# Dense up projection with upper part and remainder as one 512-column moving operand, halves added outside TensorE

## The chip, the cores and the metric

One core of a Trainium2 chip runs the whole program in one launch. The metric is device time in microseconds, the median of several executions of the same kernel. Engines are called by their row names: PE (TensorE, the matmuls), PEld (its weight loads), DVE (VectorE), ACT (ScalarE), POOL (GpSimd), SP (SyncE, which issues the weight DMAs).

## The reference, cut to what matters

All data are float32. A two-layer network (with a mixture of experts in its second layer) is followed by a second two-layer network with conditioned norms. Each dense feed-forward stage, five in all, computes

```
def swiglu(h, wg, wu, wd):
    return (jax.nn.silu(h @ wg) * (h @ wu)) @ wd      # D_MODEL = 1024, D_FF = 2816, 256 tokens
```

and is added to the residual. In the second network the conditioning vector is itself a matrix product, `mod = silu_c @ w_ada[layer] + b_ada[layer]`.

## The kernel before

The activations lie transposed, features on the 128 partitions and the T = 256 tokens along the free axis. A product at float32 accuracy is made of three matmuls in the format fp32r: weights and activations are split into an upper part (a rounded copy) and a remainder (value minus copy), and `mm3` (L1697 to L1699) adds upper x upper, upper x remainder and remainder x upper in PSUM. Each of the three has its own weight load, although the first two load the same block `w_hi`.

A dense feed-forward stage is `ffn(f, n)`, with f = 0, 2, 3, 4, 5 (f = 1 would be the experts, which have code of their own). It goes over n = FF = 22 chunks of 128 hidden features. One weight tile of 3072 columns per chunk (2048 for gate and up, 1024 for down) comes from HBM into a ring of four (`ring`), issued by SP when `tile_used` is raised. Per chunk c:

- PE: `up(c)` makes 8 blocks k x 2 (g = gate, up) x 3 = 48 matmuls of 256 columns into one PSUM bank (4 or 5, in turns; gate in columns 0 to 255, up in 256 to 511), and raises `gu_ready`. It is followed by `down(c - 1)`, 8 x 3 = 24 matmuls of 256 columns into banks 0 to 3, which waits for `hid_ready` of chunk c - 1. The order is up(0), up(1), down(0), up(2), down(1), ..., up(21), down(20), down(21). `up(c)` also waits for the split weights of its tile and for `hid_ready` of chunk c - 2, which frees its bank.
- ACT, strictly in program order: L892 copies the upper part of the gate and up weights for chunk c + 1 (in the last chunk L596, `head`, does so for the next stage, where the order asks for it); L901 copies that of the down weights for chunk c, once down(c - 2) is done; L906 waits for `gu_ready` and writes silu of the gate half from PSUM to `sg`.
- DVE, in program order: L1391 (in the last chunk L1048) subtracts for the remainder of the gate and up weights, after L892; L1400 for that of the down weights; then, in f = 0, 2, 3 and 4, blocks of the conditioning product (L1382, one row of 1024 each, with an accumulator read): none in chunk 0, one in each of chunks 1 to 4, two in each of chunks 5 to 20, none in chunk 21; then it waits for `sg_ready`, L1411 multiplies silu by the up half read from PSUM, L1415 copies the result to `hid_hi`, and L1417 subtracts for `hid_lo` and raises `hid_ready`.
- POOL issues the loads of the conditioning rows, each when its slot of four is free.

`sm` is one buffer of four rows of 256: rows 0 and 1 are `sg`, rows 2 and 3 `hid`. After the last chunk come `modulation` (small DVE operations on the finished conditioning), `residual` (DVE adds Y to xT as pairs of blocks of down(21) finish), and the next `norm` (ACT squares, POOL sums, PE sums over partitions in bank 6, called SS).

Of the kernel before, what the change touches and what calls it, by code (L numbers as in the profile page):

```python
# [22 lines left out]
P = 128  # L23
T = 256
D = 1024
KB = D // P
# [81 lines left out]
def build(nc, x_in, wstream, astream, crow, wpool, wrouter, vectors, consts, out):  # L108
# [6 lines left out]
    with ctx:  # L115
        def sb(name, shape, dtype=fp32):
            return ctx.enter_context(nc.sbuf_tensor(name, shape, dtype))
# [8 lines left out]
        xT = sb("xT", [P, KB, T])  # L126
        hT = sb("hT", [P, KB, T])
        cat = hT
        a_hi = sb("a_hi", [P, KB, T], fp32r)
        a_lo = sb("a_lo", [P, KB, T], fp32r)  # L130
        sq = sb("sq", [P, KB, T])
        proj = sb("proj", [P, 21, T])
        branch = sb("branch", [P, 3 * 4 * (16 + T)])
# [102 lines left out]
        normed = sem("normed")  # L236
        h_ready = sem("h_ready")
        gu_ready = sem("gu_ready")
        sg_ready = sem("sg_ready")
        hid_ready = sem("hid_ready")  # L240
        in_ready = sem("in_ready")
# [93 lines left out]

        def chunks_before(f):

# [244 lines left out]
        def _(act):  # L585
# [294 lines left out]
            def ffn(f, n):  # L880
                base, stage = chunks_before(f), FFN_STAGE[f]
                q0, i0 = SPLITS[stage], STARTS[stage]

                def chunk(c, r=0, last=False):

                    s, nx = (i0 + c) % NS, (i0 + c + 1) % NS
                    rt_ = 16 // NS
                    if c and not last:

                        act.wait_ge(gu_ready, r + (base + c))  # L890
                        act.wait_ge(tile_in[nx], r * rt_ + 16 * ((i0 + c + 1) // NS + 1))
                        nc.scalar.activation(w_hi[:, (q0 + c + 1) % 2, 0:UP], ring[:, nx, 0:UP], ACT.Copy)\  # L892
                            .then_inc(hi_ready, 1)
                    if last and f in NORM_AFTER:
                        act.wait_ge(gu_ready, base + c)
                        for half in range(2 if HEADS[NORM_AFTER[f]] in FFN_STAGE else 1):
                            head(NORM_AFTER[f], half, unused=False)

                    act.wait_ge(split_used, r + (q0 + c - 1))
                    act.wait_ge(tile_in[s], r * rt_ + 16 * ((i0 + c) // NS + 1))  # L900
                    nc.scalar.activation(w_hi[:, (q0 + c) % 2, UP:TILE], ring[:, s, UP:TILE], ACT.Copy)\  # L901
                        .then_inc(hi_ready, 1)
                    act.wait_ge(gu_ready, r + (base + c + 1))
                    if base + c >= 2:
                        act.wait_ge(hid_ready, r + (base + c - 1))
                    nc.scalar.activation(sg[:, c % 2, :], ps[:, 4 + c % 2, 0:T], ACT.Silu)\  # L906
                        .then_inc(sg_ready, 1)

                lead, rounds = ffn_loop(n)
                for c in range(lead):  # L910
                    chunk(c)
                    if c == 0 and f in (0, 2, 3):
                        act.wait_ge(crow_in, 16 * ((0, 2, 3).index(f) + 1))
                        nc.scalar.activation(silu_row, silu_row, ACT.Silu).then_inc(silu_row_ready, 1)
                for c in range(lead, n - 1):
                    chunk(c)
                    if f == 2 and c == FINAL_AT:
                        act.wait_ge(final_ss, 1)
                        nc.scalar.activation(norm_s[:, 0, :], SS[:, T:2 * T], ACT.Sqrt, scale=1.0 / D, bias=V("eps"))\
                            .then_inc(final_std, 1)  # L920
                chunk(n - 1, last=True)
# [117 lines left out]
        def _(dve):  # L1039
# [334 lines left out]
            def ffn(f, n):  # L1374
# [10 lines left out]
                def chunk(c, r=0, last=False, blocks=()):  # L1385

                    b = c % 2
                    if c and not last:
                        n_part = 2 * q0 + up_part(c + 1)
                        dve.wait_ge(hi_ready, r * 2 + (n_part + 1))  # L1390
                        nc.vector.tensor_tensor(w_lo[:, (q0 + c + 1) % 2, 0:UP],  # L1391
                                                ring[:, (i0 + c + 1) % NS, 0:UP],
                                                w_hi[:, (q0 + c + 1) % 2, 0:UP], ALU.subtract)\
                            .then_inc(split_ready, 1)
                    if last and f in NORM_AFTER:
                        for half in range(2 if HEADS[NORM_AFTER[f]] in FFN_STAGE else 1):
                            head(NORM_AFTER[f], half)
                    n_part = 2 * q0 + down_part(c, n)
                    dve.wait_ge(hi_ready, r * 2 + (n_part + 1))
                    nc.vector.tensor_tensor(w_lo[:, (q0 + c) % 2, UP:TILE], ring[:, (i0 + c) % NS, UP:TILE],  # L1400
                                            w_hi[:, (q0 + c) % 2, UP:TILE], ALU.subtract)\
                        .then_inc(split_ready, 1)
                    dve.wait_ge(split_ready, r * 2 + (n_part + 1))
                    dve.sem_inc(tile_used, 1)
                    for i in blocks:
                        at = b0 + i
                        ada_block(at, 0, mod_all[:, at:at + 1])
                    dve.wait_ge(sg_ready, r + (base + c + 1))

                    dve.wait_ge(split_used, r + (q0 + c - 1))  # L1410
                    nc.vector.tensor_tensor(hid[:, b, :], sg[:, b, :], ps[:, 4 + b, T:2 * T], ALU.mult)\  # L1411
                        .then_inc(hid_raw, 1)

                    dve.wait_ge(hid_raw, r + (base + c + 1))
                    nc.vector.tensor_copy(hid_hi[:, b, :], hid[:, b, :]).then_inc(hid_top, 1)  # L1415
                    dve.wait_ge(hid_top, r + (base + c + 1))
                    nc.vector.tensor_tensor(hid_lo[:, b, :], hid[:, b, :], hid_hi[:, b, :], ALU.subtract)\  # L1417
                        .then_inc(hid_ready, 1)
# [271 lines left out]
        def _(pe):  # L1690
# [363 lines left out]
            def ffn(f, n, norm_n):  # L2054
# [3 lines left out]
                def up(c, r=0):  # L2058
# [6 lines left out]
                    for k, g in [(k, g) for k in range(KB) for g in range(2)] if c < 2 else \  # L2065
                            [(k, g) for g in range(2) for k in range(KB)]:
                        if c == 0 and g == 0:
                            wait_head(norm_n, k)
                        if c == 1 and (k, g) == (0, 0):
                            pe.wait_ge(second_lo, SECOND_AT[norm_n] + 1)  # L2070
                        if c == 1 and (k, g) == (KB // 2, 0):
                            pe.wait_ge(split_ready, 2 * q0 + up_part(1) + 1)
                        at = (2 * k + g) * P
                        ins = mm3(ps[:, 4 + c % 2, g * T:(g + 1) * T], parts(stage, c, at, at + P),
                                  (a_hi[:, k, :], a_lo[:, k, :]), k == 0 and (c > 1 or g == 0), k == KB - 1)
                    ins.then_inc(gu_ready, 1)
# [373 lines left out]
```

## Time and profile before

| | us |
|---|---|
| median of 3 runs | 2694.66 (2694.05 to 2695.15) |
| the profiled execution: span from first to last instruction | 2690.4 |

The span of the profiled execution is 4.3 us below the median of the runs; what lies around the span is not in the trace. The page gives, for each engine, busy time and its share of the span; the chain that ended last; and groups of instructions by line, with the idle time of the engine before them. A timeline row gives start, duration, engine, line, operation, written and read tiles, shapes, and in brackets how long the engine sat idle before and who released it. Ends of matmuls are modelled; the distance between the starts of two neighbouring matmuls is what one costs in a stream. The granted TensorE clock is given as a share of 2.4 GHz.

### The profile page before, as it was taken

To read this page: it belongs to the slowest core of one execution; us is meant where nothing else is said; L and a number is where in the kernel's file an instruction comes from. 1 tells how busy PE (TensorE), PEld (TensorE's weight loads), DVE (VectorE), ACT (ScalarE), POOL (GpSimd) and SP (SyncE) were. 2 spreads that over 40 slices of the span, in tenths; PEclk is the share of its full clock that TensorE was granted. 3 is DMA by queue.
4 is the path that set the end of the run, shared out by engine and by line. 5 is a ranking of instruction groups with operands and counts; after the bars stand their busy time and mean duration, and the time that the engine had idled before them with its cause. 6 is when DMAs were issued, how large, how long until landed. Compare 5 with 4: busy or idle time off the path is not lost.

```text
span 2690.4 us, 48898 instructions
## 1 busy us (share of the span) xinstructions
PE 2616.0 (97%) x19438; PEld 2463.6 (92%) x19438; DVE 2068.6 (77%) x2783; ACT 1536.7 (57%) x2198; POOL 189.3 (7%) x257
## 2 busy tenths in 40 slices
PE   8999999999999999999999999998999999998999
PEld 8899988999999999999999899986999999887999
DVE  4677766988988898988889778667788787576654
ACT  4643455777777777777777633545433433445432
POOL 2001020000000000000000111012111010021000
PEclk9999998999999999999999999999999999999999
DMA  7277534998989898989899678431587577431452
GB/s 287 112 298 302 203 127 147 331 354 311 359 312 349 320 354 313 351 324 348 321 349 348 262 275 314 172 134 48 212 311 287 218 302 275 165 118 48 165 188 87
DMA packets 76822, 679.22 MB, mean 252 GB/s; under 512 B 8641, under 2 KB 8769, under 8 KB 27969
## 3 DMA queue, kind: packets, MB, share of 16 engines
q1 hardware_dynamic: 55440, 599.10, 60.0%
q0 software_dynamic: 21168, 77.08, 7.1%
q8 instruction: 158, 2.59, 0.4%
q14 instruction: 56, 0.45, 0.1%
HBM read 675.10 MB, written 1.05 MB: 251 GB/s over the span
## 4 chain that ended last, share of the span: by engine, by line
PE 85%; DVE 7%; ACT 4%; issue 2%; DMA 1%; POOL 0%; DVEq 0%; SPq 0%; ACTq 0%; POOLq 0%
PE ps L1697 23%; PE ps L1698 23%; PE ps L1699 23%; PE ps L2222 11%; PE ps L2187 1%; DVE w_parts L1462 1%; PE ps L2231 1%; PE ps L2197 1%; ACT w_parts L927 1%; DMA ring<-wstream 1%; DVE a_lo L1469 1%; DVE xT L1538 1%; ACT sq L609 1%; DVE pT L1070 1%; PE ps L1991 0%
## 5 line engine op out<-in xcount | busy, mean ns | idle before, releaser
L1697 PE MATMUL ps<-a_hi,w_parts 128*128 128x256 f32 x2544 | 727.9, 286 | 13.8 <-DVE a_lo L1089 6.3
L1698 PE MATMUL ps<-a_lo,w_parts 128*128 128x256 f32 x2544 | 720.7, 283 | 0.0
L1699 PE MATMUL ps<-a_hi,w_parts 128*128 128x256 f32 x2544 | 720.5, 283 | 0.0
L1462 DVE TENSOR_TENSOR w_parts<-ring,w_parts 128x1024 fp32r<-128x1024 f32 x448 | 547.9, 1223 | 70.2 <-ACT w_parts L927 68.4
L1697 PE MATMUL ps<-w_parts 128*128 128x256 f32 x1792 | 528.5, 295 | 0.1
L1697 PEld LDWEIGHTS ps<-a_hi,w_parts 128*128 128x128 f32 x2544 | 488.5, 192 | 24.8 <-issue 16.8
L1698 PE MATMUL ps<-w_parts 128*128 128x256 f32 x1792 | 506.1, 282 | 0.0
L1699 PE MATMUL ps<-w_parts 128*128 128x256 f32 x1792 | 505.7, 282 | 0.0
L1698 PEld LDWEIGHTS ps<-a_lo,w_parts 128*128 128x128 f32 x2544 | 488.6, 192 | 1.5 <-issue 1.4
L1699 PEld LDWEIGHTS ps<-a_hi,w_parts 128*128 128x128 f32 x2544 | 488.9, 192 | 0.0
L927 ACT ACTIVATE w_parts<-ring 128x1024 fp32r<-128x1024 f32 x448 | 472.3, 1055 | 2.0 <-DMA ring<-wstream 2.0
L1698 PEld LDWEIGHTS ps<-w_parts 128*128 128x128 f32 x1792 | 342.1, 191 | 8.6
L1697 PEld LDWEIGHTS ps<-w_parts 128*128 128x128 f32 x1792 | 340.8, 190 | 9.3 <-issue 0.3
L1699 PEld LDWEIGHTS ps<-w_parts 128*128 128x128 f32 x1792 | 341.7, 191 | 0.0
L906 ACT ACTIVATE sm<-ps 128x256 f32<-128x256 f32 x110 | 42.2, 384 | 468.1 <-PE ps L1699 467.9
L1469 DVE TENSOR_TENSOR a_lo<-ring,a_hi 128x1024 fp32r<-128x1024 f32 x224 | 273.9, 1223 | 11.8 <-ACT a_hi L934 11.1
L1391 DVE TENSOR_TENSOR w_parts<-ring,w_parts 128x2048 fp32r<-128x2048 f32 x100 | 229.3, 2293 | 59.9 <-ACT w_parts L892 59.8
L934 ACT ACTIVATE a_hi<-ring 128x1024 fp32r<-128x1024 f32 x224 | 237.6, 1061 | 52.1 <-PE ps L2222 51.9
L1698 PE MATMUL ps<-hid_lo,w_parts 128*128 128x256 f32 x880 | 249.0, 283 | 0.0
L1699 PE MATMUL ps<-hid_hi,w_parts 128*128 128x256 f32 x880 | 248.6, 282 | 0.0
L1697 PE MATMUL ps<-hid_hi,w_parts 128*128 128x256 f32 x880 | 246.7, 280 | 0.0
L1124 DVE TENSOR_TENSOR w_parts<-ring,w_parts 128x1536 fp32r<-128x1536 f32 (+1 forms) x85 | 151.2, 1812 | 101.4 <-ACT w_parts L672 97.8
(250 smaller groups left out, 4099.6 us busy)
## 6 DMA issues: line engine op xcount, KB each, us to landing
ring<-wstream SPq DMA_DIRECT2D x378, 1536.0 KB, 8.0
proj<-astream POOLq DMA_DIRECT2D x144, 512.0 KB, 6.1
cst<-consts SPq DMA_DIRECT2D x1, 1700.0 KB, 15.4
vtok<-crow POOLq DMA_DIRECT2D x3, 512.0 KB, 3.9
xT<-x_in SPq DMA_DIRECT2D x1, 1024.0 KB, 5.2
out<-xT SPq DMA_DIRECT2D x1, 768.0 KB, 3.3
proj<-wpool SPq DMA_DIRECT2D x1, 512.0 KB, 15.5
out<-xT SPq DMA_DIRECT2D x1, 256.0 KB, 3.3
```

The lines of the kernel that those rows point to most:

```text
L609: nc.scalar.activation(sq[:, k, :], xT[:, k, :], ACT.Square, scale=both[:, KB + k:KB + k + 1] if n == 5 else D ** -0.5)\
L906: nc.scalar.activation(sg[:, c % 2, :], ps[:, 4 + c % 2, 0:T], ACT.Silu)\
L927: nc.scalar.activation(up_hi[:, n % 2, half * D:(half + 1) * D], ring[:, s, half * D:(half + 1) * D], ACT.Copy).then_inc(xup_hi, 1)
L934: nc.scalar.activation(wd_hi[:, n % 2, :], ring[:, s, UP:TILE], ACT.Copy).then_inc(xdown_hi, 1)
L1124: nc.vector.tensor_tensor(w_lo[:, q, a:b], ring[:, (STARTS[stage] + i) % NS, a:b], w_hi[:, q, a:b], ALU.subtract).then_inc(split_ready, 1)
L1391: nc.vector.tensor_tensor(w_lo[:, (q0 + c + 1) % 2, 0:UP], ring[:, (i0 + c + 1) % NS, 0:UP], w_hi[:, (q0 + c + 1) % 2, 0:UP], ALU.subtract)\
L1462: nc.vector.tensor_tensor(up_lo[:, n % 2, at], ring[:, s, at], up_hi[:, n % 2, at], ALU.subtract).then_inc(xup_lo, 1)
L1469: nc.vector.tensor_tensor(wd_lo[:, n % 2, :], ring[:, s, UP:TILE], wd_hi[:, n % 2, :], ALU.subtract).then_inc(signal, 1)
L1697: mm(o, stationary[0], moving[0], start=start, stop=False, skip_group_check=True)
L1698: mm(o, stationary[0], moving[1], start=False, stop=False, skip_group_check=True)
L1699: return mm(o, stationary[1], moving[0], start=False, stop=stop, skip_group_check=True)
L2222: ins = mm(ps[:, bank + half, :], h[:, b, 0:CAP], w[:, b, half * D // 2:(half + 1) * D // 2], start=c == 0 and i == 0, stop=c == FX - 1 an ...
```

## The change

`a_hi` and `a_lo` become the two halves of one buffer `a_parts`. In four of the five dense stages (`joined(f)`, f = 0, 3, 4, 5; in f = 2 another sum uses bank 6) `up(c)` issues per block k and g one matmul of the stationary `w_hi` block with both halves, 512 columns, and one of `w_lo` with `a_hi`, 256 columns, into the first half: 16 x 2 = 32 matmuls in place of 48. Gate and up have a bank each, 4 and 5 or 6 and 7 in turns. In columns 0 to 255 of a bank stands upper x upper plus remainder x upper, in 256 to 511 upper x remainder. After `gu_ready`, ACT copies columns 256 to 511 of both banks into `sg` and `hid` (512 elements a partition); DVE adds columns 0 to 255 of both banks to them (512 elements); ACT then makes silu of `sg` in place in SBUF; DVE multiplies `sg` and `hid`, both in SBUF. The rest is as before.

```diff
-        a_hi = sb("a_hi", [P, KB, T], fp32r)
-        a_lo = sb("a_lo", [P, KB, T], fp32r)
+        a_parts = sb("a_parts", [P, 2, KB, T], fp32r)
+        a_hi, a_lo = a_parts[:, 0], a_parts[:, 1]
...
+        def joined(f):
+
+            return f != 2
+
+        def added_before(f):
+
+            return chunks_before(f) - (FF if f > 2 else 0)
+
+        def gu_bank(f, c):
+
+            return 4 + 2 * (c % 2) if joined(f) else 4 + c % 2
+
...
+                    if joined(f):
+                        act.wait_ge(gu_ready, r + (base + c + 1))
+                        if base + c >= 2:
+                            act.wait_ge(hid_ready, r + (base + c - 1))
+                        gu = ps[:, gu_bank(f, c):gu_bank(f, c) + 2, :]
+                        nc.scalar.activation(sm[:, c % 2::2, :], gu[:, :, T:2 * T], ACT.Copy).then_inc(gu_copied, 1)
+                        act.wait_ge(gu_added, r + (added_before(f) + c + 1))
+                        nc.scalar.activation(sg[:, c % 2, :], sg[:, c % 2, :], ACT.Silu).then_inc(sg_ready, 1)
+                        return
...
+                    if joined(f):
+                        dve.wait_ge(gu_ready, r + (base + c + 1))
+                        gu = ps[:, gu_bank(f, c):gu_bank(f, c) + 2, :]
+                        dve.wait_ge(gu_copied, r + (added_before(f) + c + 1))
+                        nc.vector.tensor_tensor(sm[:, b::2, :], sm[:, b::2, :], gu[:, :, 0:T], ALU.add)\
+                            .then_inc(gu_added, 1)
                     dve.wait_ge(sg_ready, r + (base + c + 1))
...
-                    nc.vector.tensor_tensor(hid[:, b, :], sg[:, b, :], ps[:, 4 + b, T:2 * T], ALU.mult)\
-                        .then_inc(hid_raw, 1)
+                    if joined(f):
+                        nc.vector.tensor_tensor(hid[:, b, :], sg[:, b, :], hid[:, b, :], ALU.mult).then_inc(hid_raw, 1)
+                    else:
+                        nc.vector.tensor_tensor(hid[:, b, :], sg[:, b, :], ps[:, 4 + b, T:2 * T], ALU.mult)\
+                            .then_inc(hid_raw, 1)
...
+                        if joined(f):
+                            hi, lo = parts(stage, c, at, at + P)
+                            bank = gu_bank(f, c) + g
+                            mm(ps[:, bank, :], hi, a_parts[:, :, k, :], start=k == 0, stop=k == KB - 1,
+                               skip_group_check=True)
+                            ins = mm(ps[:, bank, 0:T], lo, a_hi[:, k, :], start=False, stop=k == KB - 1,
+                                     skip_group_check=True)
+                            continue
```

## Rows read from the trace of the kernel before

**Rows 1.** The page: busy time by engine, and the chain that ended last

```profile
PE 2616.0 (97%) x19438; PEld 2463.6 (92%) x19438; DVE 2068.6 (77%) x2783; ACT 1536.7 (57%) x2198; POOL 189.3 (7%) x257
PE 85%; DVE 7%; ACT 4%; issue 2%; DMA 1%; POOL 0%; DVEq 0%; SPq 0%; ACTq 0%; POOLq 0%
```

**Rows 2.** Windows of the joined stages: length, busy us by engine, PEclk, DMA share, GB/s

```profile
140.00:315.00 175.00, 175.00 (x1461) 175.00 (x1461) 137.39 (x191) 64.41 (x63) 17.36 (x33) 1.00 0.76 286
2496.00:2690.00 194.00, 189.57 (x1578) 189.22 (x1577) 104.49 (x128) 72.52 (x71) 0.00 (x0) 0.99 0.41 153
```

**Rows 3.** Timeline, one chunk of f = 3, ACT: start, duration, line, [idle <- releaser]

```profile
2030.00 0.38 ACT L906 ACTIVATE sm<-ps 128x256 f32<-128x256 f32 x1 [4.69 <-PE ps L1699]
2030.28 1.91 ACT L892 ACTIVATE w_parts<-ring 128x2048 fp32r<-128x2048 f32 x1
...
2038.63 0.38 ACT L906 ACTIVATE sm<-ps 128x256 f32<-128x256 f32 x1 [4.69 <-PE ps L1699]
```

**Rows 4.** Timeline, the same chunk, DVE

```profile
2030.41 0.42 DVE L1411 TENSOR_TENSOR sm<-sm,ps 128x256 f32<-128x256 f32 x1 [0.87 <-ACT sm L906]
2030.87 0.29 DVE L1415 CAST hid_hi<-sm 128x256 fp32r<-128x256 f32 x1
2031.20 0.42 DVE L1417 TENSOR_TENSOR hid_lo<-sm,hid_hi 128x256 fp32r<-128x256 f32 x1
2032.22 2.29 DVE L1391 TENSOR_TENSOR w_parts<-ring,w_parts 128x2048 fp32r<-128x2048 f32 x1 [0.60 <-ACT w_parts L892]
2034.43 1.22 DVE L1400 TENSOR_TENSOR w_parts<-ring,w_parts 128x1024 fp32r<-128x1024 f32 x1
2035.80 1.23 DVE L1382 SCALAR_TENSOR_TENSOR proj<-proj,vtok 128x1024 f32<-128x1024 f32 x1
...
2038.09 0.08 DVE L1382 DVE_READ_ACCUMULATOR proj<-proj,vtok 128x1 f32 x1
```

**Rows 5.** Timeline, PE, matmuls of 256 columns: up ends, down(c - 1), next up

```profile
2038.43 0.28 PE L1697 MATMUL ps<-hid_hi,w_parts 128*128 128x256 f32 x1
...
2041.31 0.28 PE L1697 MATMUL ps<-a_hi,w_parts 128*128 128x256 f32 x1
...
2047.07 0.28 PE L1697 MATMUL ps<-hid_hi,w_parts 128*128 128x256 f32 x1
```

**Rows 6.** Timeline, PE, matmuls of 512 columns in the experts, six in a row

```profile
1272.97 0.63 PE L2222 MATMUL ps<-a_hi,hid_hi 128*128 128x512 f32 x2
1273.44 0.63 PE L2222 MATMUL ps<-a_lo,hid_hi 128*128 128x512 f32 x2
1273.91 0.63 PE L2222 MATMUL ps<-a_hi,hid_lo 128*128 128x512 f32 x2
1274.37 0.81 PE L2231 MATMUL ps<-proj,pT 128*128 128x256 f32 x3
```

**Rows 7.** Timeline, PE, matmuls of 384 columns: the first and last of seven

```profile
1806.33 0.33 PE L1697 MATMUL ps<-w_parts,a_hi 128*128 128x384 f32 x1
...
1807.37 0.33 PE L1697 MATMUL ps<-w_parts,a_hi 128*128 128x384 f32 x1
```

**Rows 8.** Groups by line and form: count, busy us, mean ns, idle before

```profile
L956 ACT ACTIVATE w_parts<-ps 128x512 fp32r<-128x512 f32 x16 | 9.5, 591 | 7.7 <-PE ps L2187 7.7
L803 ACT ACTIVATE a_hi<-hT 128x256 fp32r<-128x256 f32 x32 | 12.6, 416 | 24.0 <-DVE hT L1207 23.9
L1267 DVE TENSOR_TENSOR branch<-ps,cst 128x512 f32<-128x512 f32 x12 | 8.3, 690 | 9.0 <-PE ps L1818 7.7 <-DVE w_parts L1124 1.1
```

**Rows 9.** Timeline, DVE, last chunk of f = 0

```profile
310.11 0.42 DVE L1411 TENSOR_TENSOR sm<-sm,ps 128x256 f32<-128x256 f32 x1 [3.40 <-ACT sm L906]
```

**Rows 10.** Windows at idle stretches of PE and behind them, columns as in rows 2

```profile
73.80:76.10 2.30, 0.20 (x3) 0.08 (x4) 1.73 (x4) 2.30 (x10) 0.00 (x0) 1.00 0.00 0
76.70:80.10 3.40, 3.40 (x15) 2.59 (x16) 2.01 (x2) 3.39 (x11) 0.00 (x0) 0.50 0.02 5
...
376.60:378.80 2.20, 0.09 (x3) 0.02 (x2) 1.62 (x4) 2.20 (x10) 0.00 (x0) 1.00 0.01 4
378.80:382.20 3.40, 3.40 (x28) 2.59 (x28) 2.03 (x2) 3.40 (x8) 0.00 (x0) 1.00 0.00 0
...
423.30:426.20 2.90, 0.03 (x1) 0.00 (x0) 2.29 (x3) 2.83 (x5) 0.00 (x0) 1.00 0.00 0
428.30:431.70 3.40, 3.40 (x17) 3.40 (x17) 3.40 (x5) 0.37 (x1) 0.00 (x0) 0.50 0.02 5
```

**Rows 11.** Timeline, DVE, remainders of the activations for up(0) of f = 0

```profile
125.36 0.42 DVE L1094 TENSOR_TENSOR a_lo<-hT,a_hi 128x256 fp32r<-128x256 f32 x1
...
126.09 0.42 DVE L1094 TENSOR_TENSOR a_lo<-hT,a_hi 128x256 fp32r<-128x256 f32 x1
```

More of the change, by code:

```diff
@@ L238, in build @@
         gu_ready = sem("gu_ready")
+        gu_copied = sem("gu_copied")
+        gu_added = sem("gu_added")
         sg_ready = sem("sg_ready")
```

## The prediction, blind

> **What bounds the kernel now.** I read the page first: PE is busy for 97% of the span and carries 85% of the chain that ended last [rows 1]. That is an average, so I next took the stretches of the joined stages. In them PE is busy throughout, while DVE is busy 137 of 175 us in a stage with conditioning blocks and 104 of 194 us in f = 5, which has none [rows 2]. DVE has room on average; the reader is to see that the room differs by stage. Then I laid out one chunk. Silu starts of neighbouring chunks are 8.63 us apart [rows 3]. PE goes from the start of down(c - 1) through the next up to the following down in the same 8.64 us, without a hole: 72 matmuls at 0.120 us, 2.88 us of down and 5.76 us of up [rows 5]. So PE sets the pace. Its margins are short in one place: DVE finishes the second conditioning block at 2038.17, only 0.46 us before the next silu starts at 2038.63 [rows 3, 4]. ACT begins the next weight copy 0.28 us after silu starts, and not before, as the copy stands behind silu in its order [rows 3].
>
> **What PE saves.** Per block and gate three matmuls of 256 columns, 3 x 119.9 = 359.7 ns, become one of 512 and one of 256. Six matmuls of 512 columns in a row took 1.40 us, 233 ns each [rows 6]. Those of 384 columns took 1.04 us for six, 173 ns each [rows 7]: 13 ns over their 160 ns of columns at 2.4 GHz, as those of 256 are 13 ns over 107. By that the 512 would cost 227 ns. I take 232, near the direct row, so the pair costs 352 ns and saves 7.7 ns; the bounds are 347 (saving 13) and 360 (saving none, if a moving operand in two pieces costs more than one in one piece, which no row shows; I keep a loss beyond that out, because the 256-column matmul is unchanged). Below, I also price 336, a 512 with no extra beyond its columns. At 16 pairs a chunk the saving is 0.12 us, so the PE pace becomes 8.51 us; over 22 chunks 2.7 us per stage, over four stages 10.8 us. Up(0) doesn't give it, since the remainders of the activations come every 0.73 us [rows 11] and a k takes 0.72 already: 4 x 0.12 = 0.5 us less, of which the stages limited by DVE feel little; I charge 0.3.
>
> Section "Back-to-back issue gap" of the Trainium skill's page "TensorE: Matmul & The Clock Gate" gives an isolated matmul its columns over 2.4 GHz plus 2.5 ns: 216 ns for 512, 109 ns for 256. By that the three cost 328 ns and the pair 325 ns, an estimate from the page of a saving of only 3 ns. The trace disagrees with the page on both sizes (120 and 233 ns).
>
> **What ACT and DVE get.** Per chunk ACT gains a copy of 512 elements from PSUM, 0.591 us (the nearest row of that shape), and its silu now reads SBUF, 0.416 for 0.38. DVE gains an addition of 512 elements with PSUM, 0.690 us [rows 8]; its product of two SBUF operands stays at 0.42, as L1417 does [rows 4]. Work alone would fit, but the order matters. Before, the path from up's end to hid_ready was silu, product, cast, subtraction: 1.62 us from the silu's start [rows 3, 4]. Now it is 0.59 + 0.03, 0.69 + 0.03, 0.42 + 0.04, 0.46, 0.33 and 0.42: 3.0 us. The 0.03 is what such a hand-over takes (silu ends at 2030.38, the product starts at 2030.41). In the middle of a stage this is hidden: down(c) starts a whole pace later.
>
> **The loop that the addition closes.** Silu now waits for an addition on DVE, and DVE comes to it only behind the two conditioning blocks of that chunk; the next weight copy on ACT waits behind silu; L1391 on DVE waits for that copy; the blocks of the next chunk stand behind L1391. Before, silu waited for PE alone, so DVE could be late without delaying ACT. Once around: addition 0.69 + 0.03; silu start to weight copy start 0.32 (its 0.42 less the 0.10 of overlap that rows 3 show); copy 1.91 + 0.03; L1391 to L1400 2.21; L1400 to first block 1.37; two blocks 2.29 to the accumulator read, with which the next DVE instruction may start [rows 3, 4]. The sum is 8.85 us. That is 0.34 above the new PE pace and 0.22 above the old one. With one block once around takes 7.70, with none (f = 5) 6.55, so only chunks 5 to 20 of f = 0, 3 and 4 fall behind.
>
> DVE falls behind by 16 x 0.34 = 5.5 us in such a stage. The cover is the distance from hid_ready to down's start: 8.51 less the 3.0 of the path, less 0.20 by which silu starts behind the matmul that follows up [rows 3, 5], less about 0.15 for PE to pick up: 5.15 us. The split weights for up(c + 2) have about the same cover. So PE stands some 0.3 us inside the stage. In the last chunk there are no blocks, and DVE regains 8.51 - 6.55 = 2.0 us; before, it waited 3.40 us there [rows 9]. It is then still about 3.2 us late. Only down(20), 2.88 us, lies between up(21) and down(21), and even an undelayed path needs 0.20 + 3.0 + 0.15 = 3.35 us, 0.4 to 0.5 more than that. PE thus waits about 3.5 us ahead of down(21). Each such stage comes to -2.7 + 0.3 + 3.5 = +1.1 us. In f = 5 it is -2.7 + 0.4 = -2.3 us. Sum so far: 3 x 1.1 - 2.3 + 0.3 = +1.3 us.
>
> **The clock.** A wait of 3.5 us is longer than any now in the trace. The 2.1 us of idle before 76.1 and the 2.9 us before 426.2 were followed by stretches at a granted clock of 0.50 (1.2 GHz), about 0.6 and 2 us after PE had begun again; a like 2.1 us before 378.8 was not [rows 10]. Behind the new wait stands down(21), 2.88 us of dense matmuls, and then the norm. If the clock falls 0.6 to 2 us into it, 0.9 to 2.3 us of that work doubles; the most is half of a 3.4 us stretch, 1.7 us. I take 1.2 per stage, 3.6 in all, with 0 and 5.1 as bounds.
>
> **Costs at nothing.** The conditioning loads on POOL and the ring loads on SP are raised by DVE up to 5.3 us later, but a tile is loaded nearly three paces ahead and DMA is at 76% [rows 2]; if the loads were short, ACT would show waits on `ring`. The table load for silu (it now lies between copy and silu in chunk 0) delays chunk 0, whose hidden part is needed only after up(1). The strided write of `sm` and two more semaphores: nothing. Stage f = 2 and the experts are untouched.
>
> **The forecast.** +1.3 + 3.6 = +4.9 us: 2690.4 becomes 2695.3 in the span, and 2694.66 becomes 2699.6 in the median.
>
> **Rivals.**
> - *The loop as above, but the clock holds.* The 2.1 us before 378.8 speak for it, the length of the new wait against. 2694.66 + 1.3 = 2696.0; at 347 ns a pair (+0.6 a stage with blocks, -4.25 in f = 5) 2692.5.
> - *Slower: the loop is longer than 8.85.* Once the cover is used up, each 0.05 us more costs 3 x 16 x 0.05 = 2.4 us. Its place is the two new hand-overs and the two 512-element reads of PSUM while PE writes beside them; for it speaks that no row shows ACT and DVE reading banks in this way, against it that all its terms are rows with spreads of 0.01 us. At 9.0 us: +4.9 + 7.2, so 2706.8. It is outside 0.2% from 8.86 on.
> - *No saving on PE* (the change doesn't do what it says). With the pair at 360 the sum is 3 x 1.6 + 0.4 + 0.3 = +5.6, with the clock +9.2: 2703.9. By the Trainium skill's 3 ns (pair at 357) it would be 3 x 1.4 - 0.7 + 0.3 = +3.8, with the clock +7.4: 2702.1. Rows 6 speak against both.
> - *Faster: the extra time of a matmul is its weight load, and goes under the 512 columns.* Pair at 336, clock holding: +0.4 in each limited stage, -8.0 in f = 5, +0.3: -6.5, 2688.2. For it: one weight load in three goes. Against: 384 columns still pay 13 ns. Only f = 5 can gain, as the loop holds the others.
>
> **How the numbers follow.** Chances: forecast 0.46, clock holds 0.19, loop longer 0.17, no saving 0.12, faster 0.06. A measurement tells about 0.2%, 5.4 us, from no change. The forecast at +4.9 lies just inside it, with bounds that go over it (1.3 + 5.1 = +6.4), so I split it 0.29 to 0.17; clock holds goes inside; loop longer to slower; of no saving 0.02 lies inside. Faster 0.06, same 0.50, slower 0.44. The range from 2691.5 to 2708.0 leaves out the faster rival, and above it the loop longer than 9.03.
>
> **What would show it.** Right: starts of 512 and 256 in up 232 and 120 ns apart; silu starts 8.85 us apart in the later chunks of f = 0, 3, 4, and 8.51 in f = 5; PE idle about 3.5 us before down(21) in those three and about 0.4 in f = 5; the granted clock at 0.5 right behind. Wrong: silu starts at PE's pace in all stages (a shorter loop, and some -9 us), or waits of up and down from chunk 10 on (a longer one).

## The result and the profile after

The changed kernel takes 2702.82 us (median of 6 runs, 2701.67 to 2705.79) against 2694.68 us of the kernel before in the same rounds (6 runs, 2692.24 to 2695.72): ratio 1.0031, 95% interval 1.002 to 1.0043. It is slower by 8 us. The forecast was 2699.6 with a range of 2691.5 to 2708.0; the time lies in the range, but "within 0.2%" was given the most and "slower" came. The profiled execution has a span of 2700.4 us, 10.0 longer than before. First the page of the kernel after, the same two parts as in [rows 1].

```profile
PE 2611.9 (97%) x18030; PEld 2391.1 (89%) x18030; DVE 2125.4 (79%) x2871; ACT 1578.9 (58%) x2286; POOL 190.3 (7%) x257
...
PE 67%; DVE 19%; ACT 8%; issue 5%; DMA 1%; POOL 0%; DVEq 0%; ACTq 0%; SPq 0%; POOLq 0%
```

The busy shares hardly moved; the chain did. There are 1408 matmuls fewer, PE's share of the chain went down from 85% to 67%, and DVE's up from 7% to 19%. The next view is one chunk in f = 3 of the kernel after, first ACT, then DVE, as in [rows 3, 4].

```profile
2041.24 0.42 ACT L924 ACTIVATE sm<-sm 128x256 f32<-128x256 f32 x1 [5.19 <-DVE sm L1435]
2041.56 1.90 ACT L906 ACTIVATE w_parts<-ring 128x2048 fp32r<-128x2048 f32 x1
2043.37 1.04 ACT L915 ACTIVATE w_parts<-ring 128x1024 fp32r<-128x1024 f32 x1
2044.31 0.58 ACT L922 ACTIVATE sm<-ps 128x512 f32<-128x512 f32 x1
2050.08 0.42 ACT L924 ACTIVATE sm<-sm 128x256 f32<-128x256 f32 x1 [5.20 <-DVE sm L1435]
```

```profile
2040.52 0.68 DVE L1435 TENSOR_TENSOR sm<-sm,ps 128x512 f32<-128x512 f32 x1
2041.69 0.43 DVE L1441 TENSOR_TENSOR sm<-sm 128x256 f32<-128x256 f32 x1 [0.48 <-ACT sm L924]
...
2043.49 2.29 DVE L1414 TENSOR_TENSOR w_parts<-ring,w_parts 128x2048 fp32r<-128x2048 f32 x1 [0.59 <-ACT w_parts L906]
2045.70 1.22 DVE L1423 TENSOR_TENSOR w_parts<-ring,w_parts 128x1024 fp32r<-128x1024 f32 x1
2047.07 1.23 DVE L1405 SCALAR_TENSOR_TENSOR proj<-proj,vtok 128x1024 f32<-128x1024 f32 x1
...
2048.22 1.22 DVE L1405 SCALAR_TENSOR_TENSOR proj<-proj,vtok 128x1024 f32<-128x1024 f32 x1
2049.36 0.08 DVE L1405 DVE_READ_ACCUMULATOR proj<-proj,vtok 128x1 f32 x1
2049.36 0.68 DVE L1435 TENSOR_TENSOR sm<-sm,ps 128x512 f32<-128x512 f32 x1
```

L1435 is the addition, L924 silu, L922 the copy out of PSUM, L906 and L1414 the upper part and the remainder of the next gate and up weights. Silu used to wait 4.69 us for PE [rows 3]. Now it waits 5.2 us for the addition on DVE, and the addition starts the moment the second conditioning block is done, without any idle time. From addition to addition 8.84 us pass. By the starts of these rows that is once around the loop: addition to silu 0.72, silu to weight copy 0.32, copy to L1414 1.93, L1414 to L1423 2.21, L1423 to the first block 1.37, and two blocks to the next addition 2.29. PE would need 8.43 (e2_pe_part_alone below).

To see where the 10 us arise I took the length of each stage from the traces, from the first matmul of its up(0) to the first matmul behind the next norm, less the same in the kernel before (us; f = 0 is 197.55 us there). In brackets stands what the 24 matmuls of down(21) took beyond the 2.76 us of the kernel before, at a lower granted clock, contained in the number ahead of it.

| kernel | f = 0 | f = 3 | f = 4 | f = 5 | all other stretches |
|---|---|---|---|---|---|
| after | +5.6 (2.3) | +4.3 (1.4) | +3.6 (1.6) | -3.6 | +0.1 |
| e1_blocks_behind_add | -3.5 | -3.4 | -3.6 | -3.6 | +6.0 |
| e2_pe_part_alone | -4.2 | -4.1 | -4.3 | -4.1 | +0.8 |
| e3_three_matmuls | +4.7 (1.6) | +3.1 | +2.3 | +0.6 | +4.7 |
| e4_filled_wait | +4.8 | +5.2 | +3.9 | -3.6 | +2.3 |
| e5_row_first | +6.0 (1.6) | +5.3 (1.1) | +3.6 (1.4) | -3.6 | +3.7 |
| e7_filled_seven | +3.3 | +3.1 | +2.4 | -3.7 | +3.1 |
| e8_one_each_side | -3.5 | -3.4 | -3.6 | -3.6 | +5.2 |
| e9_copy_ahead_of_silu | -3.4 | -3.3 | -3.2 | -3.2 | +2.2 |
| e10_row_behind_copies | +6.5 (2.3) | +4.9 (1.1) | +3.5 (1.4) | -3.6 | +2.6 |
| e11_row_and_its_wait | +3.8 (1.5) | +3.3 (1.4) | +4.5 (2.3) | -3.7 | +5.3 |
| e12_three_one_each_side | +0.5 | +0.6 | +0.5 | +0.5 | -1.5 |

The last column is code that no kernel changed. It varies by 7.5 us from trace to trace, so the table is read by its stages. The four stages added up meet the difference of the medians within 3 us in every kernel but e3_three_matmuls, where the median is 5 us higher than they say; what made those 5 us was not found.

### The profile page after: what moved, and what is told of

Read it like the earlier page. It is cut to its first block, busy times and chain, and to the rows that moved or that the text cites. A ratio compares the mean times of both kernels' runs of the same rounds, so it can differ in the third digit from the quotient of the medians.

```text
span 2700.4 us, 46346 instructions
## 1 busy us (share of the span) xinstructions
PE 2611.9 (97%) x18030; PEld 2391.1 (89%) x18030; DVE 2125.4 (79%) x2871; ACT 1578.9 (58%) x2286; POOL 190.3 (7%) x257
## 4 chain that ended last, share of the span: by engine, by line
PE 67%; DVE 19%; ACT 8%; issue 5%; DMA 1%; POOL 0%; DVEq 0%; ACTq 0%; SPq 0%; POOLq 0%
PE ps L1729 15%; PE ps L1730 15%; PE ps L1731 15%; PE ps L2262 11%; DVE w_parts L1414 4%; PE ps L2109 4%; ACT w_parts L906 4%; DVE w_parts L1423 2%; DVE proj L1405 2%; PE ps L2111 2%; DVE sm L1435 1%; PE ps L2227 1%; DVE w_parts L1494 1%; PE ps L2271 1%; PE ps L2237 1%
## 5 line engine op out<-in xcount | busy, mean ns | idle before, releaser
L2109 PE MATMUL ps<-a_parts,w_parts 128*128 128x512 f32 x1408 | 496.4, 395 | 4.1 <-DVE a_parts L1112 3.4
L2111 PE MATMUL ps<-a_parts,w_parts 128*128 128x256 f32 x1408 | 394.0, 280 | 0.0
L1729 PE MATMUL ps<-a_parts,w_parts 128*128 128x256 f32 x1136 | 327.6, 288 | 10.1 <-DVE a_parts L1112 3.1
L1730 PE MATMUL ps<-a_parts,w_parts 128*128 128x256 f32 x1136 | 321.5, 283 | 0.0
L1731 PE MATMUL ps<-a_parts,w_parts 128*128 128x256 f32 x1136 | 321.3, 283 | 0.0
L2109 PEld LDWEIGHTS ps<-a_parts,w_parts 128*128 128x128 f32 x1408 | 263.9, 187 | 64.1 <-issue 6.2
L1501 DVE TENSOR_TENSOR a_parts<-ring,a_parts 128x1024 fp32r<-128x1024 f32 x224 | 273.9, 1223 | 11.5 <-ACT a_parts L957 10.9
L1414 DVE TENSOR_TENSOR w_parts<-ring,w_parts 128x2048 fp32r<-128x2048 f32 x100 | 229.2, 2292 | 63.1 <-ACT w_parts L906 63.1
L957 ACT ACTIVATE a_parts<-ring 128x1024 fp32r<-128x1024 f32 x224 | 237.5, 1060 | 50.5 <-PE ps L2262 50.3
L2111 PEld LDWEIGHTS ps<-a_parts,w_parts 128*128 128x128 f32 x1408 | 265.8, 189 | 0.0
L1729 PE MATMUL ps<-hid_hi,w_parts 128*128 128x256 f32 x880 | 252.8, 287 | 12.3 <-DVE hid_lo L1449 10.1
L2262 PE MATMUL ps<-a_parts,hid_hi 128*128 128x512 f32 x896 | 248.6, 399 | 11.4 <-DVE hid_lo L1586 10.9
L1731 PE MATMUL ps<-hid_hi,w_parts 128*128 128x256 f32 x880 | 251.1, 285 | 0.0
```

The lines of the kernel that those rows point to most:

```text
L957: nc.scalar.activation(wd_hi[:, n % 2, :], ring[:, s, UP:TILE], ACT.Copy).then_inc(xdown_hi, 1)
L1414: nc.vector.tensor_tensor(w_lo[:, (q0 + c + 1) % 2, 0:UP], ring[:, (i0 + c + 1) % NS, 0:UP], w_hi[:, (q0 + c + 1) % 2, 0:UP], ALU.subtract)\
L1501: nc.vector.tensor_tensor(wd_lo[:, n % 2, :], ring[:, s, UP:TILE], wd_hi[:, n % 2, :], ALU.subtract).then_inc(signal, 1)
L1729: mm(o, stationary[0], moving[0], start=start, stop=False, skip_group_check=True)
L1730: mm(o, stationary[0], moving[1], start=False, stop=False, skip_group_check=True)
L1731: return mm(o, stationary[1], moving[0], start=False, stop=stop, skip_group_check=True)
```

## The experiments

All are edits of the changed kernel.

**e2_pe_part_alone.** PE's part without its price: copy and addition are left out, and with them the term upper x remainder of the result.

```diff
-                        nc.scalar.activation(sm[:, c % 2::2, :], gu[:, :, T:2 * T], ACT.Copy).then_inc(gu_copied, 1)
-                        act.wait_ge(gu_added, r + (added_before(f) + c + 1))
-                        nc.scalar.activation(sg[:, c % 2, :], sg[:, c % 2, :], ACT.Silu).then_inc(sg_ready, 1)
+                        nc.scalar.activation(sg[:, c % 2, :], ps[:, gu_bank(f, c), 0:T], ACT.Silu)\
+                            .then_inc(sg_ready, 1)
...
-                        nc.vector.tensor_tensor(sm[:, b::2, :], sm[:, b::2, :], gu[:, :, 0:T], ALU.add)\
-                            .then_inc(gu_added, 1)
...
-                        nc.vector.tensor_tensor(hid[:, b, :], sg[:, b, :], hid[:, b, :], ALU.mult).then_inc(hid_raw, 1)
+                        nc.vector.tensor_tensor(hid[:, b, :], sg[:, b, :], ps[:, gu_bank(f, c) + 1, 0:T], ALU.mult)\
+                            .then_inc(hid_raw, 1)
```

> Only PE's part of the change: matmuls of 512 and 256 columns, but ACT and DVE as in the kernel before (silu and product read columns 0 to 255 of the two banks; no copy, no addition, and the term upper x remainder in columns 256 to 511 is left out of the result). It measures the saving by itself. Loop theory: nothing else stood in the way, so each of the four stages is 21 x 16 x 0.013 = 4.4 us shorter: 2694.7 - 17.5 = 2677. Rival (a 512-column matmul saves less in a long stream than the rows show, 7.7 ns a pair): 2694.7 - 10.3 = 2684.

Measured: 2676.93 us, ratio 0.9939 (0.9922 to 0.9955), as expected. Silu starts are 8.43 us apart in all four stages; each is 4.1 to 4.3 us shorter. The pair is worth 13 ns, not 7.7. The timeline of PE in the kernel after shows how, two pairs from f = 4:

```profile
2119.70 0.40 PE L2109 MATMUL ps<-a_parts,w_parts 128*128 128x512 f32 x1
2119.94 0.28 PE L2111 MATMUL ps<-a_parts,w_parts 128*128 128x256 f32 x1
2120.05 0.40 PE L2109 MATMUL ps<-a_parts,w_parts 128*128 128x512 f32 x1
2120.28 0.28 PE L2111 MATMUL ps<-a_parts,w_parts 128*128 128x256 f32 x1
2120.40 0.40 PE L2109 MATMUL ps<-a_parts,w_parts 128*128 128x512 f32 x1
```

From pair to pair 0.35 us pass. Over the whole stage a 512-column matmul takes 230 ns and the 256-column one behind it 117 ns from start to start (medians; the means are 234 and 117).

**e3_three_matmuls.** ACT's and DVE's part without the saving of PE.

```diff
-                            mm(ps[:, bank, :], hi, a_parts[:, :, k, :], start=k == 0, stop=k == KB - 1,
+                            mm(ps[:, bank, 0:T], hi, a_hi[:, k, :], start=k == 0, stop=False,
+                               skip_group_check=True)
+                            mm(ps[:, bank, T:2 * T], hi, a_lo[:, k, :], start=False, stop=k == KB - 1,
```

> Only ACT's and DVE's part: copy, addition and silu in SBUF as in the changed kernel, but the 512-column matmul is undone into two of 256 into the same columns, so PE's pace is 8.63 again. Loop theory: f = 0, 3 and 4 are held by the loop of 8.85 us and hardly notice, at most 0.7 us each; f = 5 loses its 4.4 us: 2702.8 + 4.4 + about 0.5 = 2708, with silu starts still 8.85 apart. Rival (PE still sets the pace and the loss is in waits at the ends): each of the four stages loses 4.4 us, 2702.8 + 17.5 = 2720.

Measured: 2710.46 us, ratio 1.0064 (1.0047 to 1.008). The stage without blocks loses its whole gain (from -3.6 to +0.6), the three with blocks lose nothing (+4.7, +3.1, +2.3 for +5.6, +4.3, +3.6). They are even shorter, as the clock fell in one of them only: without the numbers in brackets they are +3.1, +3.1 and +2.3 for +3.3, +2.9 and +2.0. Silu stays at 8.85 us. PE doesn't set the pace of f = 0, 3 and 4.

**e1_blocks_behind_add.** The loop is opened on DVE: the conditioning blocks of a chunk are done behind the addition.

```diff
+                        for i in blocks:
+                            at = b0 + i
+                            ada_block(at, 0, mod_all[:, at:at + 1])
                     dve.wait_ge(sg_ready, r + (base + c + 1))
```

The same three lines ahead of the addition are left to f = 2 alone.

> The changed kernel with one edit: in the joined stages DVE does the conditioning blocks of a chunk behind the addition instead of ahead of it. Work and counts are the same. Loop theory (silu waits for an addition that stands behind two blocks, and the weight copy stands behind silu): the two blocks (2.3 us) leave the loop, which falls from 8.85 to about 8.1 us (addition 0.7, blocks 2.3, product, cast and subtraction 1.1, L1414 2.2, L1423 1.4, waits about 0.3), under PE's pace of 8.43. All four stages then run at 8.43, PE waits 0.4 to 0.5 us before the last down, the clock doesn't fall, and each stage is 3.9 us shorter than in the kernel before: 2694.7 - 15.6 = 2679. Rival theory (ACT and DVE have too much work in all, or their reads of PSUM hold up PE, in whatever order): the time stays within 3 us of the changed kernel's 2702.8.

Measured: 2681.49 us, ratio 0.9952 (0.9936 to 0.9969). All work of the change is still there, only its order on DVE differs, and the kernel is 21 us faster than the changed one. The timeline of e1 in f = 0, ACT and DVE:

```profile
204.81 0.60 ACT L922 ACTIVATE sm<-ps 128x512 f32<-128x512 f32 x1 [3.83 <-PE ps L2115]
206.24 0.42 ACT L924 ACTIVATE sm<-sm 128x256 f32<-128x256 f32 x1 [0.82 <-DVE sm L1436]
...
213.25 0.60 ACT L922 ACTIVATE sm<-ps 128x512 f32<-128x512 f32 x1 [3.83 <-PE ps L2115]
```

```profile
205.51 0.69 DVE L1436 TENSOR_TENSOR sm<-sm,ps 128x512 f32<-128x512 f32 x1 [0.99 <-ACT sm L922]
206.12 1.22 DVE L1405 SCALAR_TENSOR_TENSOR proj<-proj,vtok 128x1024 f32<-128x1024 f32 x1
```

ACT's copy waits for PE again, DVE's addition has 0.99 us to spare, and the pace is 8.44.

**e8_one_each_side** leaves the first block ahead of the addition and puts the second behind it (`blocks[:1]` and `blocks[1:]` in the two loops of e1).

> The changed kernel with the first conditioning block of a chunk ahead of the addition, as it was, and only the second, in chunks 5 to 20, behind it. Loop theory: once around is the addition 0.69 + 0.03, silu 0.32, weight copy 1.94, L1414 2.21, L1423 1.37, one block 1.15, that is 7.7 us on ACT's side; on DVE's side, blocks and all, 8.1 to 8.2. Both are under 8.43, so the chunks with two blocks run at PE's pace, PE waits about 0.5 us before the last down, and the time is that of e1_blocks_behind_add, 2681.5, within 3 us. Rival (what matters is how far hid_ready comes behind the matmuls, not the loop; here it is as late as in the changed kernel): 2700.

Measured: 2680.01 us, ratio 0.9947 (0.9932 to 0.9962). The lateness at the start of the stage (silu starts 8.72, 7.70, 7.70, 7.70, 7.74, 7.70, 7.90 us apart in f = 0) goes away by chunk 7, and from there it is 8.43.

**e9_copy_ahead_of_silu** cuts the loop on the other engine: on ACT the copy of the next weights goes ahead of silu.

```diff
-                    if c and not last:
+                    if c and not last and not joined(f):
...
+                        if c < n - 2:
+                            nn = (i0 + c + 2) % NS
+                            act.wait_ge(tile_in[nn], r * rt_ + 16 * ((i0 + c + 2) // NS + 1))
+                            nc.scalar.activation(w_hi[:, (q0 + c + 2) % 2, 0:UP], ring[:, nn, 0:UP], ACT.Copy)\
+                                .then_inc(hi_ready, 1)
                         act.wait_ge(gu_added, r + (added_before(f) + c + 1))
```

> The loop is cut at its other link: the conditioning blocks stay ahead of the addition, but on ACT, in the joined stages, the copy of the next weights stands between the copy of the PSUM columns and silu, so it no longer waits for the addition. Loop theory: DVE then goes around in its own work and one wait for silu, addition 0.72, silu 0.45, product to subtraction 1.13, L1414 2.21, L1423 1.37, blocks 2.3, 8.2 us in all, under 8.43. PE sets the pace of all four stages: 2694.7 - 14 to - 15.6, about 2680. Rival (DVE's blocks ahead of the addition are late in themselves, whatever ACT does): 8.85 stays, 2700 or more.

Measured: 2681.02 us, ratio 0.9954 (0.9939 to 0.9969), silu 8.43 apart. In its trace (f = 0, ACT, then DVE) the weight copy is L926 and silu L929, and the addition L1440 still follows the second block without idle time:

```profile
203.96 0.60 ACT L922 ACTIVATE sm<-ps 128x512 f32<-128x512 f32 x1 [4.49 <-PE ps L2116]
204.46 1.91 ACT L926 ACTIVATE w_parts<-ring 128x2048 fp32r<-128x2048 f32 x1
206.26 0.41 ACT L929 ACTIVATE sm<-sm 128x256 f32<-128x256 f32 x1
```

```profile
204.11 1.22 DVE L1410 SCALAR_TENSOR_TENSOR proj<-proj,vtok 128x1024 f32<-128x1024 f32 x1
205.26 0.08 DVE L1410 DVE_READ_ACCUMULATOR proj<-proj,vtok 128x1 f32 x1
205.26 0.69 DVE L1440 TENSOR_TENSOR sm<-sm,ps 128x512 f32<-128x512 f32 x1
```

Blocks ahead of the addition do no harm if the weight copy doesn't wait for silu. Either cut is enough; it takes both links to make the loop.

**e12_three_one_each_side** joins the edits of e3 and e8.

> ACT's and DVE's part of the change alone, as in e3_three_matmuls (three matmuls of 256 columns, PE's pace 8.63), and with one conditioning block on each side of the addition, as in e8_one_each_side. Loop theory: with the loop at 7.7 to 8.2 us the copy, the addition and the later silu cost only the wait of 0.47 us and 0.1 us ahead of and in each stage's last down: 4 x 0.6 = 2.4 us, 2694.7 + 2.4 = 2697, silu starts 8.63 apart. Rival (the added work itself costs the 15.8 us between e3_three_matmuls and the kernel before): 2707 to 2711.

Measured: 2696.5 us, ratio 1.0013 (1.0004 to 1.0022); each stage 0.5 to 0.6 us longer. That is the whole price of copy, addition and later silu once the loop is open. Against it stand 4.2 us a stage from PE.

**e4_filled_wait** and **e7_filled_seven** keep PE at work in its wait ahead of down(21), with 12 and with 7 idle matmuls whose result nothing uses. The edit of e7:

```diff
                 down(n - 2)
+                if joined(f) and f != 5:
+                    for _ in range(7):
+                        mm(ps[:, 4, 0:T], ones[:, :], C("cos"), start=True, stop=True)
                 down(n - 1)
```

> The changed kernel, and in f = 0, 3 and 4 PE does 12 idle matmuls (ones by a constant, float32, 256 columns, 0.216 us each, 2.6 us) into the free bank 4 between down(20) and down(21), within the wait of 3.0 to 3.6 us. Clock theory: the granted clock stays at 1 through down(21), whose 24 matmuls again take 2.75 us from first to last start in place of 5.08, 4.18 and 4.34: 2702.8 - 5.3 = 2697.5. Rival (the clock falls for what comes after, or the slow matmuls are hidden by residual and norm): under 1 us from 2702.8.

Measured: 2705.7 us, ratio 1.0049 (1.0033 to 1.0066), a miss of 8 us: I had sized a float32 matmul by one record. PE came 1.5 us late out of the filling (down(21) of f = 0 starts at 316.73, in the changed kernel at 315.28).

> As e4_filled_wait with 7 idle matmuls in place of 12. The 12 took 5.2 us, not 2.6 (a float32 matmul is two records of 0.216 us), and so were 1.5 us too long, but the clock stayed at 1 and the 24 matmuls of down(21) took 2.94 us from first to last start. Seven take 3.0 us and fit the waits of 3.0 to 3.6 us. Clock theory: down(21) is back at about 2.9 us in f = 0, 3 and 4 (5.08, 4.18, 4.34 in the changed kernel), 4.9 us in all, and nothing is late: 2702.8 - 4.9 = 2698. Rival (the slow matmuls were hidden by residual and norm): 2702 to 2703.

Measured: 2700.22 us, ratio 1.0024 (1.0014 to 1.0034). The windows over down(21) of f = 0 (columns as in [rows 2]), first the second half of it in the kernel after, then all of it in e7:

```profile
318.00:321.40 3.40, 3.40 (x15) 3.24 (x15) 2.10 (x6) 1.81 (x6) 2.06 (x3) 0.50 0.10 43
```

```profile
315.50:318.40 2.90, 2.89 (x24) 2.89 (x24) 2.66 (x17) 1.41 (x4) 0.58 (x1) 1.00 0.95 407
```

The three stages are 2.3, 1.3 and 1.2 us shorter than in the changed kernel, 4.8 in all where 4.9 were expected. The median fell by 2.6 only; in this trace unchanged stretches took 3.0 us more than in that of the changed kernel, among them 1.6 in the stretch from f = 0 to f = 2, which holds the experts, and 1.3 in the mixer ahead of f = 3, each with a fall of the clock of its own.

**e5_row_first, e10_row_behind_copies, e11_row_and_its_wait** ask why f = 0 and 3 lose more than f = 4. Each moves the silu of the conditioning row: ahead of chunk 0; into chunk 1 behind the weight copies; and there with DVE's wait for it moved as well.

```diff
                     if joined(f):
+                        if c == 1 and f in (0, 3):
+                            act.wait_ge(crow_in, 16 * ((0, 2, 3).index(f) + 1))
+                            nc.scalar.activation(silu_row, silu_row, ACT.Silu).then_inc(silu_row_ready, 1)
                         act.wait_ge(gu_ready, r + (base + c + 1))
...
+                    if c == 1 and f in (0, 3):
+                        dve.wait_ge(silu_row_ready, min(ADA_FFN.index(f), 2) + 1)
                     for i in blocks:
```

> The changed kernel, but in f = 0 and 3 the silu of the conditioning row (L937, 1.05 us on ACT, between silu of chunk 0 and the next weight copy) is done ahead of chunk 0, and the table load with it. In the trace of the changed kernel silu starts of chunks 0 and 1 are 8.72 us apart there and 7.77 in f = 4, and the loop never catches up with PE. Theory: this is the term that the sum lacked; those two stages are held by the loop from chunk 0 to 21, so all that is taken from it counts in full, 1.0 for the row and about 0.6 for the table load, 1.6 us in each: 2702.8 - 3.2 = 2699.6. Rival (the stages are held only from chunk 13 or so on, as the sum said): the early lateness is made up in chunks 1 to 4, and the time stays within 1 us of 2702.8.

Measured: 2707.62 us, ratio 1.0054 (1.004 to 1.0067), a miss of 8 us. Silu of chunks 0 and 1 did come 7.77 us apart, but the row ahead of chunk 0 delayed the first silu of f = 0 by 2.5 us (136.08 for 133.59).

> e5_row_first put the silu of the conditioning row ahead of chunk 0, where ACT had no room either: the first silu of the chunk came 2.5 us later (136.08 for 133.59), and of that 1.5 us were still there at the last silu of the stage, so whatever delays the head of the loop is never made up, but the edit didn't take the row out of the loop's way. Here the row (1.05 us) stands in chunk 1 behind the two weight copies, where ACT waits over 4 us for the addition. Theory: it leaves the path; in f = 0 and 3 silu of chunks 0 and 1 start 7.77 us apart in place of 8.72, and the whole 0.95 us is still gone at the last silu of the stage, 179.0 us from the first in place of 179.97 in f = 0; 1.9 us in all, 2702.8 to 2700.9, within what the clock does elsewhere. Rival (the early lateness is made up in chunks 1 to 4): first to last silu stays at 179.97.

Measured: 2706.9 us, ratio 1.0048 (1.0035 to 1.0061), a miss for the reason told in the next expectation; the row of DVE that shows it:

```profile
137.96 2.29 DVE L1417 TENSOR_TENSOR w_parts<-ring,w_parts 128x2048 fp32r<-128x2048 f32 x1 [2.48 <-ACT vtok L920]
```

> e10_row_behind_copies lengthened the loop instead of shortening it: DVE's wait for the row stands ahead of the whole of chunk 1, so L1417 began at 137.96, 1.9 us after the weight copy it needs had ended; silu of chunks 0 and 1 came 9.59 us apart (8.72 in the changed kernel), and the 0.87 us were all there at the last silu, 180.84 us after the first for 179.97. Here the wait is moved too, to just ahead of the first conditioning block of chunk 1. Theory: silu of chunks 0 and 1 of f = 0 and 3 start 7.77 us apart, first to last silu is 179.0 us in f = 0, and the time is 1.9 us under that of the changed kernel, 2701, if the clock does the same elsewhere. Rival (an early gain is lost in PE's waits of chunks 13 to 20): first to last silu stays at 179.97.

Measured: 2701.88 us, ratio 1.0031 (1.002 to 1.0042). In the trace it is as expected: silu of chunks 0 and 1 starts 7.78 us apart, first to last silu of f = 0 takes 179.05 us (179.97 in the changed kernel), and without the clock f = 0 and 3 come to +2.3 and +1.9, as f = 4 does (+2.0 in the changed kernel). The median can't show 1.9 us; it moved by 0.9. What is taken from or added to the head of the loop (-0.9 here, +0.9 in e10_row_behind_copies) is there in full at the last silu.

## Why the prediction was right in kind and short in size

Step by step:

- **The loop.** Forecast 8.85 us, measured 8.84 to 8.85 in chunks 5 to 20 of all three stages, but for one step of 8.89 in f = 0 (into chunk 5) and one of 9.20 in f = 3 (into chunk 9, where DVE stood idle for 0.49 us ahead of the first block; why was not looked for). With one block it took 7.70 (forecast 7.70), with none 6.62 (6.55). Its terms came from rows of other lines: addition 0.68 (forecast 0.69), silu 0.42. That the blocks and the weight copy are its two links is shown by e1_blocks_behind_add, e8_one_each_side and e9_copy_ahead_of_silu.
- **The wait ahead of down(21).** Forecast about 3.5 us; PE in the kernel after, at the end of f = 0:

```profile
315.28 0.58 PE L1729 MATMUL ps<-hid_hi,w_parts 128*128 128x256 f32 x1 [3.47 <-DVE hid_lo L1449]
315.66 0.41 PE L1730 MATMUL ps<-hid_lo,w_parts 128*128 128x256 f32 x1
315.87 0.41 PE L1731 MATMUL ps<-hid_hi,w_parts 128*128 128x256 f32 x1
```

  PE was idle for 3.5 us in f = 0 and 4 and for 2.9 in f = 3, where the last step of the loop took 6.0 us. In f = 5 it was idle for 0.30 us; by the starts, down(21) came 0.46 us late (forecast 0.4).
- **The start of the stage: the step that failed.** The prediction lets PE wait 0.3 us inside a stage with blocks. "DVE falls behind by 16 x 0.34 = 5.5 us", against a cover of 5.15, counts from chunk 5, as if DVE were level with PE there. It isn't. Compare chunk 4 of f = 0 with chunk 4 of f = 5, where nothing is late: the last matmul of up(4), then silu.

```profile
161.62 0.28 PE L2111 MATMUL ps<-a_parts,w_parts 128*128 128x256 f32 x1
165.40 0.42 ACT L924 ACTIVATE sm<-sm 128x256 f32<-128x256 f32 x1 [2.87 <-DVE sm L1435]
```

```profile
2545.65 0.28 PE L2111 MATMUL ps<-a_parts,w_parts 128*128 128x256 f32 x1
2547.39 0.42 ACT L924 ACTIVATE sm<-sm 128x256 f32<-128x256 f32 x1 [0.82 <-DVE sm L1435]
```

  Silu starts 3.78 us behind the matmul in the first and 1.74 in the second, so it is 2.0 us late before the first chunk with two blocks; in f = 3 it is 2.0 and in f = 4 1.1 us late. Up(1) follows up(0) directly and ends 5.6 us after it, while the loop takes 8.72 us in f = 0 and 3 and 7.77 in f = 4. The difference of these two is the silu of the row on ACT, which I had not put in the sum. Chunks 2 to 4 make up only 0.73 us each. So the cover is used up sooner: from down(12) on in f = 0 and 3, and from down(14) on in f = 4, PE goes at the pace of the loop, 8.84 for 8.43 us. (The rows show up to 0.14 us of idle time ahead of a down; the rest is spread over the matmuls around it.) By down(20) it has lost 3.6, 3.7 and 2.6 us where the sum had 0.3. Of that the late start is 2.0, 2.0 and 1.1; some 1.1 come from PE being faster than forecast (16 chunks in which it runs ahead of the loop by 0.41 and not 0.34), so that most of what PE saves beyond the forecast is given back as waiting. Stages without the clock: +3.3, +2.9 and +2.0 us for +1.1 each, 4.9 us too little. e10_row_behind_copies and e11_row_and_its_wait show that lateness at the head isn't made up; the part of it that f = 4 has too was read from the trace and not taken out by a run.
- **What PE saves.** 7.7 ns a pair forecast, 13 measured. The bound of 347 ns that I gave, from the rows of 384 columns, was the right value, though not by its parts: it took 227 ns for the 512 columns and left the 256 at 120, and the stream shows 230 and 117. The row of 512 columns stands among matmuls of the experts that are 233 ns apart for a reason I didn't look for. The larger saving brought f = 5 to -3.6 us for -2.3. In the three others it brought nothing, since the loop sets their length.
- **The clock.** 1.2 us a stage forecast, 2.3, 1.4 and 1.6 measured, 5.3 in all for 3.6, just over the upper bound of 5.1. That bound took one stretch of 3.4 us at half the clock. In f = 0 the granted clock was 0.50 (1.2 GHz) from 314.6 to 321.4, over all of down(21), with 0.21 us between matmuls; the trace of the kernel before already had a longer stretch, from 428.3 to 445.3. It also had a longer wait of PE than the new one, 8.3 us at the start of the program. e7_filled_seven shows that the idle PE is the cause: with PE at work in the wait, down(21) is back at its length. A wait doesn't always bring it: in e3_three_matmuls the one of 2.96 us was followed by a fall, those of 2.78 and 2.10 us were not.
- **The sum.** +4.9, plus 4.9 for the start, plus 1.7 for the clock, less 1.3 for f = 5, less 0.3 charged for up(0): +9.9. The spans differ by 10.0, the medians by 8.1. The time of a run lies 1.7 us above its span throughout, so the profiled execution of the kernel before, with 2690.4, was some 2.6 us below its median. That the median came within 3.3 us of the forecast is in part luck: the terms were 6.6 us too low on one side and 1.6 too high on the other, and the median shows 1.8 less than the stages.
- **The rivals.** The clock holding, the loop longer than 8.85, no saving on PE, and faster: none of them came. (The pair of 336 ns in the last has the 512 columns at 216; columns alone are 213, so "no extra" would be 333.) The slower one named the right end for the wrong reason; the hand-overs and the reads of PSUM took what the rows said. The Trainium skill's figure for isolated matmuls ("TensorE: Matmul & The Clock Gate", "Back-to-back issue gap"), a saving of 3 ns by my estimate, is not what the traces show: 13 ns.

The chance of 0.50 for "within 0.2%" rested on a sum of +4.9 that lay at the edge of it, with a term missing on one side. Three kernels that compute the whole result beat both: e8_one_each_side (2680.0), e9_copy_ahead_of_silu (2681.0) and e1_blocks_behind_add (2681.5) lie within each other's spread, 13 to 15 us below the kernel before, and 3 to 5 us above e2, which leaves the additions out.

## What to carry to other kernels

When an operation of one engine is made to wait for another engine, write down what is queued behind the waiter and what is queued ahead of the one it waits for, and go around once: if that closes a loop, its length competes with the pace of the bounding engine, whatever the busy shares say, and moving one queued operation past the hand-over can be worth more than the edit itself. Add up the start of the stage chunk by chunk as well; a slack per chunk in the middle is not a slack that exists at the end. A wait of the matmul engine is paid a second time if the granted clock falls behind it, here with 1.4 to 2.3 us for waits of 2.9 to 3.5.

## What the runs showed of the hardware

- In a stream that alternates 512 and 256 columns the two took 230 and 117 ns by their starts (medians), 347 ns a pair, where three of 256 took 360. Less the columns at 2.4 GHz that leaves 27 ns for the two and 40 for the three. The extra of some 13 ns per matmul seems to belong to the matmul and not to its length: one matmul fewer saved 13 ns (e2).
- A float32 matmul of 256 columns leaves two records, 0.215 us apart: seven of them are the fourteen in this row of e7 (timeline, PE).

```profile
311.87 3.19 PE L2146 MATMUL ps<-cst,ones 128*128 128x256 f32 x14
```

- In unchanged stretches the granted clock falls in other places from kernel to kernel. The stretch from the end of f = 0 to the start of f = 2, which holds the experts, took between 0.7 us less (e12) and 4.6 us more (e11) than in the kernel before. Whether the moment within the run or chance decides that was not tried. It may be why medians differ from what the stages add up to; that is not shown.
